# Two interleaved slabs whose last operand tile comes last in a two-block transformer kernel, and the fourth norm's squares summed two tiles later

## The chip, the cores and the metric

The program runs on one NeuronCore of a Trainium2 chip, as one launch. The metric is its device time in microseconds (us), from which a median of several executions is given. The profile is of one execution, and its span reaches from the first to the last instruction of the program. The engines are called as the profile calls them: PE is TensorE (its weight loads are PEld), DVE is VectorE, ACT is ScalarE, SP issues the DMAs of the weights.

## What is computed

Two transformer-like blocks, one after the other, on 512 tokens of width 1024, in float32. Cut to what matters here:

```python
# block 1
h = rmsnorm(x, norm_mix_pre); proj = h @ w_in
y_attn = sliding_window_attention(q, k, v, sinks, rel_bias) @ w_attn_branch
z = gelu(s5_ssm(u, ...)); z = z * sigmoid(z @ w_glu)
y_ssm = z @ w_ssm_branch
merged = sigmoid(g_attn) * y_attn + sigmoid(g_ssm) * y_ssm
x = x + rmsnorm(merged @ w_out, norm_mix_post)
h = rmsnorm(x, norm_mlp_pre)
x = x + rmsnorm(square(relu(h @ w_ff_in)) @ w_ff_out, norm_mlp_post)
# block 2
xn = rmsnorm(x, norm_mix_g_2)       # LRU branch, banded attention, gates
x = x + merged_2 @ w_out_2
xn2 = rmsnorm(x, norm_ffn_g_2)      # the fourth norm, "n4"
x = x + (silu(gate) * up) @ w_ffn_out_2
return rmsnorm(x, norm_final_g_2)
```

## The kernel before

All activations lie transposed, with channels on the 128 partitions and the 512 tokens along the free axis, in chunks of 128 channels. Every float32 product is made of three fp32r matmuls, high by high, high by low and low by high, so every operand exists as a rounded high part and a low part that holds the rest. `a_hi`/`a_lo` and `h_hi`/`h_lo` hold the activations, eight chunks each; ACT writes the high part and DVE, behind it, the low part and a count on `h_lo_ready` or `a_lo_ready`.

Weights stream in as 232 slabs of 128 by 1024 (eight 128x128 tiles). SP loads a slab into `raw`, ACT rounds it to `w_hi` (L475), DVE writes the rest to `w_lo` (L897). The pair of these is called `split`. Four slabs are in flight (`RING`), and ACT may round slab n once PE has finished slab n-4 (`half_done`).

`gemm` is PE's basic step: it waits for the slab's `w_lo`, then for the PSUM bank of its output to be free, then goes through the tiles, three matmuls of 128x512 each (L1556, L1557, L1558). With `ready` it waits ahead of each tile for that chunk of the operand. An output's bank is one of the two of `gp`, in turn. It is free when the engine that reads the output before last has counted up `out_read`; `freed_by(name, k)` is the count that has to be reached. That counter is one for the whole program and rises in program order. An operand chunk is often made from an output itself: the last chunk's low part is written at the end of a chain of PE output, DVE, ACT, DVE.

Three places matter here.

- `branch_s` (the multiplication by `w_ssm_branch`, four slabs with two outputs of four tiles each). Its operand is z times a sigmoid, from the two slabs of `glu` ahead of it. DVE makes a chunk with L1218, which also counts the bank of that `glu` output as read, and its low part with L941. Afterwards DVE and ACT work on each output in turn: L1225 (DVE, reads the bank), L1228 (DVE), L683 (ACT), L934 (DVE), and per slab one `split`. The next stage, `out`, uses the results.
- `ff`, part 0 of 4. Eight slabs (eight outputs) give the hidden chunks, each by L1293 (DVE, reads the bank, counts `out_read`), L1282 (DVE), L709 (ACT, high part), L941 (DVE, low part). The first four outputs were made together in a stage ahead (`START = 4`). Then eight slabs multiply these eight chunks, the first of them with `ready`; in part 0 their outputs are copied out by DVE at L1307.
- `n4`, the fourth norm. Squares of x are summed on ACT (L486) and DVE (L911), and PE sums them over partitions in two steps of four tiny matmuls, `first_squares` (L1579) for the first seven chunks and `last_square` (L1586) for the last. Both are done inside the first slab of `ff2`, after its tile 4. Then ACT takes the root (L494), DVE the reciprocal (L923), and PE spreads it (L1613) after tile 0 of the second slab.

DVE and ACT run in program order, so a late instruction holds up those behind it.

Of the kernel before, what the change touches and what calls it, by code (L numbers as in the profile page):

```python
# [25 lines left out]
P = 128  # L26
D = 1024
T = 512
DC = D // P
# [13 lines left out]
FF1_PART = 8  # L43
# [6 lines left out]
RING = 4  # L50
# [23 lines left out]
SLAB, _n = {}, 0  # L74
# [4 lines left out]
COUNT = dict(_counts)  # L79
# [45 lines left out]
def build(nc, slabs, params, s5p, s5bt, s5b, s5c, bias1, nd2, x_in, out):  # L125

    ctx = ExitStack()
    with ctx:
        def sb(name, shape, dt=F32):
            return ctx.enter_context(nc.sbuf_tensor(name, shape, dt))  # L130

        def sem(name):
            return ctx.enter_context(nc.semaphore(name))
# [3 lines left out]
        w_hi = sb("w_hi", [P, RING, TILES * P], F32R)  # L137
        w_lo = sb("w_lo", [P, RING, TILES * P], F32R)
# [110 lines left out]
        w_lo_ready = sem("w_lo_ready")  # L249
        half_done = sem("half_slab_done")  # L250
        out_read = sem("output_read")
# [4 lines left out]
        h_val, h_hi_ready, h_lo_ready = sem("h_value"), sem("h_hi_ready"), sem("h_lo_ready")  # L256
# [42 lines left out]
        H_AT = {"z": 0, "y1": 3, "last_z": 11, "z2": 12, "ff": 16, "xn": 48, "n4": 56}  # L299
# [45 lines left out]
        def bank(name, k):  # L345
            tensor, i = PLACE[OUT[name] + k]
            return tensor[:, i, :]

        def freed_by(name, k):

            return FREED[OUT[name] + k]
# [5 lines left out]
        class Attention:  # L357
# [3 lines left out]
            def __init__(self, first, chunk0, pairs, back, forth, q, kt, k0, v0, vt, logit, pt, sinks, name):  # L361
                self.units = [(b, pp, hp) for b in range(T // P) for pp in range(pairs) for hp in range(2)]
                self.u0, self.q, self.kt, self.k0, self.v0, self.vt = first, q, kt, k0, v0, vt
                self.logit, self.pt, self.sinks, self.name, self.pairs = logit, pt, sinks, name, pairs
                self.units_of_logit = 1.0 if name else 8.0
                self.chunks, self.done = [], []
                g = chunk0
                for b, _, _ in self.units:
                    js = [(j, b - back + j) for j in range(back + forth + 1) if 0 <= b - back + j < T // P]
                    self.chunks.append([(g + n, j, kb) for n, (j, kb) in enumerate(js)])  # L370
                    g += len(js)
                    self.done.append(g)
# [1167 lines left out]
        def _(pe):  # L1540
            def gemm(name, k, tiles, outs, x_hi, x_lo, ready=None, first=None, then={}):


                n = SLAB[name] + k
                pe.wait_ge(w_lo_ready, n + 1)
                for e in range(outs):
                    m = (outs * k if first is None else first) + e
                    dst = bank(name, m)
                    if freed_by(name, m) > 0:
                        pe.wait_ge(out_read, freed_by(name, m))  # L1550
                    for t in range(tiles):
                        if ready:
                            ready(t)
                        cols = slice((e * tiles + t) * P, (e * tiles + t + 1) * P)
                        hi, lo = w_hi[:, n % RING, cols], w_lo[:, n % RING, cols]
                        pe.matmul(dst, hi, x_hi(t), start=t == 0, stop=False)  # L1556
                        pe.matmul(dst, hi, x_lo(t), start=False, stop=False)  # L1557
                        ins = pe.matmul(dst, lo, x_hi(t), start=False, stop=t == tiles - 1)  # L1558
                        if t in then:
                            then[t]()  # L1560
                    ins.then_inc(half_done, 2 // outs)

            def a(t):
                return a_hi[:, t, :]

# [3 lines left out]
            def h(t):  # L1569
                return h_hi[:, t, :]  # L1570

            def hl(t):
                return h_lo[:, t, :]

            def first_squares(kind):

                pe.wait_ge(sq_added, ADDS * (BY_VEC[kind] + 1))
                for b in range(T // P):
                    pe.matmul(mp[:, 5, b:b + 1], ssum[:, b * P:(b + 1) * P], ones[:, 0:1], start=b == 0, stop=False,  # L1579
                              skip_group_check=True)  # L1580

            def last_square(kind):

                pe.wait_ge(sq_done, 8 * NORM[kind] - PAIRED + DC)
                for b in range(T // P):
                    ins = pe.matmul(mp[:, 5, b:b + 1], sq[(DC - 1) % 2][:, b * P:(b + 1) * P], ones[:, 0:1], start=False,  # L1586
                                    stop=True, skip_group_check=True)
                ins.then_inc(rms_sum, 1)

            def mean_square(kind):  # L1590
                first_squares(kind)
                last_square(kind)
# [16 lines left out]
            def spread(kind):  # L1609

                pe.wait_ge(rms_inverted, NORM[kind] + 1)
                for b in range(T // P):
                    ins = pe.transpose(mp[:, 5, b * P:(b + 1) * P], by_token[:, b:b + 1].to_broadcast([P, P]), ident)  # L1613
                ins.then_inc(rms_spread, 1)

            def a_stage(name, k, ready=None, then={}):
                gemm(name, k, 8, 1, a, al, ready, then=then)

            def start_stage(name, kind, count, together=DC, then={}, at_hand=()):

                order = list(at_hand)
                order += [(c, e) for c in range(len(order) // count, together) for e in range(count)]
                order += [(c, e) for e in range(count) for c in range(together, DC)]
                for c, e in order:
                    if e == 0:
                        pe.wait_ge(a_lo_ready, A_AT[kind] + c + 1)
                    if c == 0:
                        pe.wait_ge(w_lo_ready, SLAB[name] + e + 1)
                        if freed_by(name, e) > 0:
                            pe.wait_ge(out_read, freed_by(name, e))  # L1630
                    place, cols = (SLAB[name] + e) % RING, slice(c * P, (c + 1) * P)
                    hi, lo = w_hi[:, place, cols], w_lo[:, place, cols]
                    pe.matmul(bank(name, e), hi, a(c), start=c == 0, stop=False)  # L1633
                    pe.matmul(bank(name, e), hi, al(c), start=False, stop=False)  # L1634
                    ins = pe.matmul(bank(name, e), lo, a(c), start=False, stop=c == DC - 1)  # L1635
                    if c == DC - 1:
                        ins.then_inc(half_done, 2)
                        if e in then:
                            then[e]()
# [148 lines left out]
            pe.wait_ge(h_lo_ready, H_AT["last_z"] + 1)  # L1788
            for j in range(COUNT["glu"]):
                gemm("glu", j, 4, 2, lambda t: h(4 + t), lambda t: hl(4 + t))  # L1790
            for j in range(COUNT["branch_s"]):
                gemm("branch_s", j, 4, 2, h, hl,
                     (lambda t: pe.wait_ge(h_lo_ready, H_AT["z2"] + t + 1)) if j == 0 else None)
            for k in range(DC):
                a_stage("out", k, a_wait("merged") if k == 0 else None,
                        then={5: lambda: first_squares("post1")} if k == DC - 1 else {})
# [6 lines left out]
            def ff1_part(p, last=False):  # L1803

                s0, h0 = PART1 * p, H_AT["ff"] + FF1_PART * p
                for k in range(0 if p else START, FF1_PART):
                    a_stage("ff", s0 + k, then={} if p or k > START else {1: lambda: spread("n2")})
                for m in range(DC):
                    gemm("ff", s0 + FF1_PART + m, FF1_PART, 1, h, hl,
                         (lambda t: pe.wait_ge(h_lo_ready, h0 + t + 1)) if m == 0 else None,  # L1810
                         then={5: lambda: first_squares("post2")} if last and m == DC - 1 else {})

# [64 lines left out]

            def ff2_part(part, chunks, s0):
                for k in range(2 * chunks):
                    then = {0: {4: lambda: mean_square("n4")}, 1: {0: lambda: spread("n4")}}.get(s0 + k, {})  # L1880
                    gemm("ff2", s0 + k, 8, 1, h, hl,
                         (lambda t: pe.wait_ge(h_lo_ready, H_AT["n4"] + t + 1)) if s0 + k == 0 else None, then=then)
                for m in range(TAIL if part == len(FF2_CHUNKS) - 1 else DC):
                    gemm("ff2", s0 + 2 * chunks + m, chunks, 1, a, al,
                         (lambda t: pe.wait_ge(a_lo_ready, A_AT["ff2"] + 8 * part + t + 1)) if m == 0 else None)
# [195 lines left out]
```

## Time and profile before

| | |
|---|---|
| median of 3 runs | 1454.9 us (1454.07 to 1456.72) |
| the profiled execution | 1453.19 us, span 1451.4 us |
| PE busy in the span | 1412.6 us, 97% |
| DVE, ACT busy | 885.8 us, 612.7 us |
| share of the chain that ended last | PE 83%, DVE 9%, ACT 5% |
| mean granted TensorE clock | 0.997 |

A PE row of a timeline gives start, duration, engine, line, operation, output and operands. Matmuls overlap, so the distance of two starts is the rate, not the duration. The bracket is the idle time of the engine ahead of the row, and what ended it.

### The profile page before, as it was taken

Reading aid. Unit: us, or ns where it says so; the run is one execution under the profiler, and the core shown is the slowest. Engines: PE = TensorE matmul, PEld = TensorE weight load, DVE = VectorE, ACT = ScalarE, POOL = GpSimd, SP = SyncE. Lnnn points to the kernel's source line nnn. Section 1 sums busy time; section 2 is a strip of 40 time slices with the busy share of each in tenths; the row PEclk is TensorE's granted clock in tenths of the full one; section 3 lists DMA queues with packets and bytes.
Section 4 is the critical chain, followed back from the end, with each engine's and each line's share of the span. In section 5 each row is a group of like instructions: output and inputs, shape, how many; then the busy total and the mean of one; then the engine's idle time right before and its main releaser. Section 6 shows DMA issues by size and latency. Waiting matters only on the chain.

```text
span 1451.4 us, 17505 instructions
## 1 busy us (share of the span) xinstructions
PE 1412.6 (97%) x7116; PEld 1139.0 (78%) x7116; DVE 885.8 (61%) x1305; ACT 612.7 (42%) x977; POOL 1.9 (0%) x7
## 2 busy tenths in 40 slices
PE   6999999999999999999998999999999999999997
PEld 5777777787788888887786777778878888888886
DVE  6987764757635355354767888579964443453446
ACT  5453553423312222132425777788553321331232
POOL 0000000000000000000000000000000000000000
PEclk9999999999999999999999999999999999999999
DMA  4222214231323323333131121323233333333223
GB/s 166 88 83 93 59 59 145 73 108 57 116 88 101 102 88 102 90 99 108 38 116 55 48 59 58 102 73 101 88 100 91 101 102 89 100 97 106 88 87 102
DMA packets 37583, 131.60 MB, mean 91 GB/s; under 512 B 4432, under 2 KB 6608, under 8 KB 37248
## 3 DMA queue, kind: packets, MB, share of 16 engines
q1 hardware_dynamic: 37152, 127.16, 28.9%
q0 software_dynamic: 352, 3.34, 0.6%
q8 instruction: 56, 0.92, 0.3%
q14 instruction: 23, 0.19, 0.0%
HBM read 128.39 MB, written 2.10 MB: 90 GB/s over the span
## 4 chain that ended last, share of the span: by engine, by line
PE 83%; DVE 9%; ACT 5%; issue 2%; DMA 1%; SPq 0%; DVEq 0%; ACTq 0%
PE gp L1556 23%; PE gp L1557 23%; PE gp L1558 23%; PE mp L1749 2%; PE mp L1760 2%; PE mp L1730 2%; ACT w_hi L475 2%; DVE w_lo L897 2%; PE mp L1633 1%; PE mp L1635 1%; PE mp L1634 1%; PE mp L1704 1%; PE mp L1675 1%; PE mp L1710 1%; PE mp L1649 0%
## 5 line engine op out<-in xcount | busy, mean ns | idle before, releaser
L1556 PE MATMUL gp<-h_hi,w_hi 128*128 128x512 f32 x944 | 370.0, 392 | 3.7 <-DVE h_lo L941 1.9
L1558 PE MATMUL gp<-h_hi,w_lo 128*128 128x512 f32 x944 | 367.5, 389 | 0.0
L1557 PE MATMUL gp<-h_lo,w_hi 128*128 128x512 f32 x944 | 367.5, 389 | 0.0
L897 DVE TENSOR_TENSOR w_lo<-raw,w_hi 128x1024 fp32r<-128x1024 f32 x202 | 246.4, 1222 | 136.4 <-ACT w_hi L475 135.9
L1556 PE MATMUL gp<-a_hi,w_hi 128*128 128x512 f32 x692 | 271.9, 393 | 1.7 <-DVE w_lo L897 1.6
L1557 PE MATMUL gp<-a_lo,w_hi 128*128 128x512 f32 x692 | 269.4, 389 | 0.0
L1558 PE MATMUL gp<-a_hi,w_lo 128*128 128x512 f32 x692 | 269.4, 389 | 0.0
L475 ACT ACTIVATE w_hi<-raw 128x1024 fp32r<-128x1024 f32 x202 | 211.3, 1050 | 136.9 <-PE gp L1558 70.5
L1556 PEld LDWEIGHTS gp<-h_hi,w_hi 128*128 128x128 f32 x944 | 177.2, 188 | 45.1 <-issue 4.1
L1558 PEld LDWEIGHTS gp<-h_hi,w_lo 128*128 128x128 f32 x944 | 177.2, 188 | 37.3
L1557 PEld LDWEIGHTS gp<-h_lo,w_hi 128*128 128x128 f32 x944 | 177.3, 188 | 36.0
L1556 PEld LDWEIGHTS gp<-a_hi,w_hi 128*128 128x128 f32 x692 | 129.9, 188 | 32.7 <-issue 3.3
L1558 PEld LDWEIGHTS gp<-a_hi,w_lo 128*128 128x128 f32 x692 | 129.9, 188 | 27.4
L1557 PEld LDWEIGHTS gp<-a_lo,w_hi 128*128 128x128 f32 x692 | 129.9, 188 | 26.2
L709 ACT ACTIVATE h_hi<-arena 128x512 fp32r<-128x512 f32 x32 | 20.3, 633 | 134.4 <-DVE arena L1282 134.4
L1488 DVE TENSOR_TENSOR arena<-gp,R 128x512 f32<-128x512 f32 x44 | 30.4, 692 | 69.0 <-PE gp L1558 68.9
L532 ACT ACTIVATE arena<-gp 128x512 f32<-128x512 f32 x41 | 24.5, 598 | 89.1 <-PE gp L1558 88.6
L863 ACT ACTIVATE a_hi<-arena 128x512 fp32r<-128x512 f32 x22 | 13.9, 633 | 99.5 <-DVE arena L1491 99.5
L1309 DVE TENSOR_TENSOR arena<-arena,gp 128x512 f32<-128x512 f32 x24 | 16.5, 687 | 63.4 <-PE gp L1558 63.4
L897 DVE TENSOR_TENSOR w_lo<-arena,w_hi 128x1024 fp32r<-128x1024 f32 x30 | 36.7, 1223 | 29.8 <-ACT w_hi L475 29.8
L626 ACT ACTIVATE arena<-arena 128x256 f32<-128x256 f32 (+2 forms) x96 | 50.0, 526 | 0.0
L860 ACT ACTIVATE arena<-arena 128x512 f32<-128x512 f32 x22 | 13.9, 632 | 83.6 <-DVE arena L1488 83.6
(279 smaller groups left out, 1576.7 us busy)
## 6 DMA issues: line engine op xcount, KB each, us to landing
raw<-slabs SPq DMA_DIRECT2D x202, 512.0 KB, 3.6
arena<-slabs SPq DMA_DIRECT2D x30, 512.0 KB, 3.6
arena<-x_in SPq DMA_DIRECT2D x4, 512.0 KB, 6.5
arena<-x_in POOLq DMA_DIRECT2D x1, 2048.0 KB, 8.3
out_t<-arena SPq DMA_DIRECT2D x8, 256.0 KB, 2.2
arena<-bias POOLq DMA_DIRECT2D x1, 1024.0 KB, 5.2
arena<-s5b SPq DMA_DIRECT2D x1, 512.0 KB, 9.4
arena<-s5c SPq DMA_DIRECT2D x1, 512.0 KB, 10.7
```

The source lines that it names most:

```text
L475: nc.scalar.activation(w_hi[:, n % RING, :], raw(n), ACT.Copy).then_inc(w_hi_ready, 1)
L532: nc.scalar.activation(dst, bank(name, m) if src is None else src, func, scale=scale).then_inc(out_read, 1)
L626: ins = nc.scalar.activation(L, L, ACT.Exp, bias=row[:, 1, h:h + 1], scale=1.0 / A.units_of_logit, accum_out=row[:, 4, h:h + 1])
L709: nc.scalar.activation(h_hi[:, k, :], fbuf[k % 2], ACT.Copy).then_inc(h_hi_ready, 1)
L897: TT(w_lo[:, n % RING, :], raw(n), w_hi[:, n % RING, :].bitcast(F32), ALU.subtract).then_inc(w_lo_ready, 1)
L1488: TT(tmp[e], take("ff2", s0 + 2 * c + e), R[:, :], ALU.mult).then_inc(out_read, 1)
L1556: pe.matmul(dst, hi, x_hi(t), start=t == 0, stop=False)
L1557: pe.matmul(dst, hi, x_lo(t), start=False, stop=False)
L1558: ins = pe.matmul(dst, lo, x_hi(t), start=False, stop=t == tiles - 1)
L1730: pe.matmul(A.scores(i)[:, lo:hi], A.q[rows, 4 * pp + h4, b * P:(b + 1) * P], A.kt[rows, A.k0 + pp, k_lo:k_hi], start=True, stop=True).the ...
L1749: ins = pe.transpose(mp[:, 3 + g % 2, h * P:(h + 1) * P], A.logit[u % 2][:, h, j * P:(j + 1) * P], ident)
L1760: ins = pe.matmul(mp[HD * p:HD * p + HD, 5, 0:2 * P], A.vt[:, pp, kb, HD * p:HD * p + HD], A.pt[:, j, 2 * P * p:2 * P * (p + 1)], start=x ...
```

## The change

Nothing is added or removed; PE's instructions are put in another order, and waits with them. A new helper `late_tile` takes two outputs together: all tiles but the last of the first, all tiles but the last of the second, then the last tile of the first and of the second. It is used for the first slab of `branch_s` (its two outputs) and, in part 0 of `ff`, for the first two of the eight slabs of the second half. Ahead of its first matmul PE waits for both slabs' `w_lo` and for both banks. In `ff2`'s first slab the two sums of squares move from behind tile 4 to behind tile 6.

```diff
+            def late_tile(places, tiles, x_hi, x_lo, ready):
+                for some in (range(tiles - 1), (tiles - 1,)):
+                    for n, m, dst, step in places:
+                        for t in some:
+                            ready(t)
+                            cols = slice((m + t) * P, (m + t + 1) * P)
+                            hi, lo = w_hi[:, n % RING, cols], w_lo[:, n % RING, cols]
+                            pe.matmul(dst, hi, x_hi(t), start=t == 0, stop=False)
+                            pe.matmul(dst, hi, x_lo(t), start=False, stop=False)
+                            ins = pe.matmul(dst, lo, x_hi(t), start=False, stop=t == tiles - 1)
+                        if t == tiles - 1:
+                            ins.then_inc(half_done, step)
...
-            for j in range(COUNT["branch_s"]):
-                gemm("branch_s", j, 4, 2, h, hl,
-                     (lambda t: pe.wait_ge(h_lo_ready, H_AT["z2"] + t + 1)) if j == 0 else None)
+            pe.wait_ge(w_lo_ready, SLAB["branch_s"] + 1)
+            pe.wait_ge(out_read, max(freed_by("branch_s", 0), freed_by("branch_s", 1)))
+            late_tile([(SLAB["branch_s"], 4 * e, bank("branch_s", e), 1) for e in range(2)], 4, h, hl,
+                      lambda t: pe.wait_ge(h_lo_ready, H_AT["z2"] + t + 1))
+            for j in range(1, COUNT["branch_s"]):
+                gemm("branch_s", j, 4, 2, h, hl)
...
-                for m in range(DC):
-                    gemm("ff", s0 + FF1_PART + m, FF1_PART, 1, h, hl,
+                k0 = s0 + FF1_PART
+                if p == 0:
+                    pe.wait_ge(w_lo_ready, SLAB["ff"] + k0 + 2)
+                    pe.wait_ge(out_read, max(freed_by("ff", k0), freed_by("ff", k0 + 1)))
+                    late_tile([(SLAB["ff"] + k0 + m, 0, bank("ff", k0 + m), 2) for m in range(2)], FF1_PART, h, hl,
+                              lambda t: pe.wait_ge(h_lo_ready, h0 + t + 1))
+                for m in range(0 if p else 2, DC):
+                    gemm("ff", k0 + m, FF1_PART, 1, h, hl,
...
-                    then = {0: {4: lambda: mean_square("n4")}, 1: {0: lambda: spread("n4")}}.get(s0 + k, {})
+                    then = {0: {6: lambda: mean_square("n4")}, 1: {0: lambda: spread("n4")}}.get(s0 + k, {})
```

PE's queue in `branch_s`, before: the last two matmuls of the first output's last tile, and the start of the second output, whose bank is waited for there.

```order
L1557 MATMUL gp<-h_lo,w_hi 128x512
L1558 MATMUL gp<-h_hi,w_lo 128x512
L1556 MATMUL gp<-h_hi,w_hi 128x512 [waits h_lo_ready,output_read]
L1557 MATMUL gp<-h_lo,w_hi 128x512
L1558 MATMUL gp<-h_hi,w_lo 128x512
```

The same place now: the second output's first tile, which is the fourth tile of the pass, begins without a wait for a bank.

```order
L1572 MATMUL gp<-h_lo,w_hi 128x512
L1573 MATMUL gp<-h_hi,w_lo 128x512
L1571 MATMUL gp<-h_hi,w_hi 128x512 [waits h_lo_ready]
L1572 MATMUL gp<-h_lo,w_hi 128x512
L1573 MATMUL gp<-h_hi,w_lo 128x512
```

The wait for the second output's bank now stands in front of the first output's first tile, 9 or more matmuls earlier. The first output ends with its 21st matmul of the pass, where it ended with its 12th.

PE's queue in `ff`, part 0, before: the end of the last tile of slab `k0` and the start of slab `k0 + 1`.

```order
L1556 MATMUL gp<-h_hi,w_hi 128x512 [waits h_lo_ready]
L1557 MATMUL gp<-h_lo,w_hi 128x512
L1558 MATMUL gp<-h_hi,w_lo 128x512
L1556 MATMUL gp<-h_hi,w_hi 128x512 [waits output_read,w_lo_ready]
L1557 MATMUL gp<-h_lo,w_hi 128x512
L1558 MATMUL gp<-h_hi,w_lo 128x512
```

Now, the start of the pass over both slabs (behind the last product of the first half).

```order
L1557 MATMUL gp<-a_lo,w_hi 128x512
L1558 MATMUL gp<-a_hi,w_lo 128x512
L1571 MATMUL gp<-h_hi,w_hi 128x512 [waits h_lo_ready,output_read,w_lo_ready]
L1572 MATMUL gp<-h_lo,w_hi 128x512
L1573 MATMUL gp<-h_hi,w_lo 128x512
```

The wait for the second slab's bank and its `w_lo` moved ahead by 24 matmuls, in front of the first slab; slab `k0` ends with the 45th matmul of the pass, where it ended with its 24th.

PE's queue in the first slab of `ff2`, before: tile 4, the two sums of squares, tile 5.

```order
L1558 MATMUL gp<-h_hi,w_lo 128x512
L1579 MATMUL mp<-par,arena 128x1 [waits square_added]
L1579 MATMUL mp<-par,arena 128x1 x3
L1586 MATMUL mp<-par,arena 128x1 [waits square_done]
L1586 MATMUL mp<-par,arena 128x1 x3
L1556 MATMUL gp<-h_hi,w_hi 128x512 [waits h_lo_ready]
```

And now, from tile 5 on.

```order
L1556 MATMUL gp<-h_hi,w_hi 128x512 [waits h_lo_ready]
L1557 MATMUL gp<-h_lo,w_hi 128x512
L1558 MATMUL gp<-h_hi,w_lo 128x512
L1556 MATMUL gp<-h_hi,w_hi 128x512 [waits h_lo_ready]
L1557 MATMUL gp<-h_lo,w_hi 128x512
L1558 MATMUL gp<-h_hi,w_lo 128x512
L1593 MATMUL mp<-par,arena 128x1 [waits square_added]
L1593 MATMUL mp<-par,arena 128x1 x3
L1600 MATMUL mp<-par,arena 128x1 [waits square_done]
L1600 MATMUL mp<-par,arena 128x1 x3
```

Tiles 5 and 6, six matmuls, moved in front of the sums (L1593 and L1600 are the same lines of code as L1579 and L1586, 14 lines further down).

## Rows read from the trace of the kernel before

**Rows 1.** The page, section 1, PE's line: busy us, share, instructions.

```profile
PE 1412.6 (97%) x7116; PEld 1139.0 (78%) x7116; DVE 885.8 (61%) x1305; ACT 612.7 (42%) x977; POOL 1.9 (0%) x7
```

**Rows 2.** Timeline of PE, `branch_s`: start us, duration us, instruction, idle before.

```profile
257.01 0.39 PE L1556 MATMUL gp<-h_hi,w_hi 128*128 128x512 f32 x1
...
258.82 0.39 PE L1558 MATMUL gp<-h_hi,w_lo 128*128 128x512 f32 x1
260.00 0.50 PE L1556 MATMUL gp<-h_hi,w_hi 128*128 128x512 f32 x1 [0.79 <-DVE h_lo L941]
...
263.56 0.39 PE L1556 MATMUL gp<-h_hi,w_hi 128*128 128x512 f32 x1
...
275.99 0.47 PE L1556 MATMUL gp<-h_hi,w_hi 128*128 128x512 f32 x1 [1.17 <-DVE arena L1225]
...
282.86 0.47 PE L1556 MATMUL gp<-a_hi,w_hi 128*128 128x512 f32 x1 [1.12 <-DVE w_lo L897]
```

**Rows 3.** Timeline of DVE, end of `glu` and `branch_s`.

```profile
257.88 0.68 DVE L1218 TENSOR_TENSOR arena<-arena 128x512 f32<-128x512 f32 x1
...
261.35 0.68 DVE L1225 SCALAR_TENSOR_TENSOR arena<-arena,gp 128x512 f32<-128x512 f32 x1
...
282.08 0.68 DVE L1225 SCALAR_TENSOR_TENSOR arena<-arena,gp 128x512 f32<-128x512 f32 x1
```

**Rows 4.** Timeline of PE, `ff` part 0, from the first to the second half.

```profile
379.94 0.39 PE L1558 MATMUL gp<-a_hi,w_lo 128*128 128x512 f32 x1
380.97 0.47 PE L1556 MATMUL gp<-h_hi,w_hi 128*128 128x512 f32 x1 [0.65 <-issue]
...
386.45 0.50 PE L1556 MATMUL gp<-h_hi,w_hi 128*128 128x512 f32 x1 [1.13 <-DVE h_lo L941]
...
393.28 0.39 PE L1558 MATMUL gp<-h_hi,w_lo 128*128 128x512 f32 x1
393.50 0.39 PE L1556 MATMUL gp<-h_hi,w_hi 128*128 128x512 f32 x1
```

**Rows 5.** Timeline of DVE, the same place.

```profile
384.39 0.68 DVE L1293 TENSOR_TENSOR arena<-gp,R 128x512 f32<-128x512 f32 x1
...
385.71 1.47 DVE L941 TENSOR_TENSOR h_lo<-arena,h_hi 128x512 fp32r<-128x512 f32 x2
...
393.70 0.69 DVE L1307 COPY arena<-gp 128x512 f32<-128x512 f32 x1 [3.20 <-PE gp L1558]
```

**Rows 6.** Windows: us, PE, PEld, DVE, ACT, POOL busy (instructions), granted clock, DMA share, GB/s.

```profile
250.00:300.00 50.00, 46.92 (x203) 37.49 (x202) 32.51 (x43) 19.93 (x28) 0.00 (x0) 1.00 0.30 90
784.00:786.00 2.00, 0.00 (x0) 0.00 (x0) 1.83 (x8) 0.87 (x2) 0.00 (x0) 1.00 0.00 0
788.00:790.00 2.00, 2.00 (x10) 1.46 (x10) 0.45 (x2) 1.73 (x3) 0.00 (x0) 0.50 0.61 139
```

**Rows 7.** Timeline of PE, second attention: the matmuls behind the longest later wait.

```profile
786.71 1.97 PE L1749 MATMUL mp<-par,arena 128*128 128x128 f32 x8 [2.86 <-DVE arena L1164]
```

**Rows 8.** Timeline of PE, the first products of the program.

```profile
21.85 0.79 PE L1633 MATMUL gp<-a_hi,w_hi 128*128 128x512 f32 x1 [3.60 <-DVE a_lo L932]
...
25.43 0.44 PE L1635 MATMUL gp<-a_hi,w_lo 128*128 128x512 f32 x1
```

**Rows 9.** Timeline of PE, first slab of `ff2`.

```profile
1081.86 1.05 PE L1579 MATMUL mp<-par,arena 128*128 128x1 f32 x8
1083.72 1.05 PE L1586 MATMUL mp<-par,arena 128*128 128x1 f32 x8 [0.82 <-ACT arena L486]
1084.64 0.48 PE L1556 MATMUL gp<-h_hi,w_hi 128*128 128x512 f32 x1
```

**Rows 10.** Timeline of ACT, the last square of `n4`.

```profile
1083.06 0.61 ACT L486 ACTIVATE arena<-arena 128x512 f32<-128x512 f32 x1
```

**Rows 11.** Timeline of DVE, the reciprocal and the low part ahead of it.

```profile
1083.18 0.75 DVE L943 SCALAR_TENSOR_TENSOR h_lo<-arena,par,h_hi 128x512 fp32r<-128x512 f32 x1 [0.79 <-ACT h_hi L848]
...
1085.79 0.17 DVE L923 RECIPROCAL arena<-arena 128x4 f32<-128x4 f32 x1
```

## Prediction

> **What bounds the kernel now.** I read the page first, then PE's waits, then the timelines of PE, DVE and ACT at the three places that the change touches. The page shows PE busy for 97% of the span [rows 1]: this kernel ends when PE has issued its matmuls, and whatever keeps PE from issuing is added to the time. The rate is seen in a run without a wait: from 257.01 to 258.82 us lie 8 steps, 0.227 us each [rows 2]; a slab of 24 matmuls takes 5.44 us. A wait costs a little more than itself: from 260.00 to 263.56 us there are 15 steps, 3.40 us by the rate and 3.56 us in the trace, so about 0.12 to 0.16 us goes on restarting; I take 0.12 [rows 2]. From the end of a DVE instruction that frees a bank to PE's next matmul it is 0.10 us: L1225 ends at 282.08 + 0.68 = 282.76, PE goes on at 282.86 [rows 2, 3]. From the start of an output's last matmul to the DVE instruction that reads it, 0.42 us (393.28 to 393.70) [rows 4, 5].
>
> The waits that the change is about are short: 0.79 us in `branch_s` for the last chunk's low part [rows 2], 1.13 us in `ff` [rows 4], 0.82 us of idle between the two sums in `ff2` [rows 9]. So all that it can win is under 3 us. Against it stands what the front of each pass now waits for.
>
> **`branch_s`: a bank that is read late, ahead of a chain that has no slack.** PE now waits, ahead of its first matmul, for the read of `glu`'s fourth output. That is counted by L1218, which ends at 257.88 + 0.68 = 258.56 us [rows 3]. PE starts at 258.66 instead of 257.01. The wait for the last chunk is gone then (18 matmuls lie ahead of it), and all 24 matmuls end at 258.66 + 0.12 + 5.44 = 264.22, against 263.56: by PE alone a loss of 0.7 us. But the first output is complete only with the 21st matmul, which starts at 258.66 + 0.12 + 20 x 0.227 = 263.32; DVE's L1225 can read it at 263.74. Before, it ran at 261.35 [rows 3], so it is late by 2.4 us. Does that matter? L1225 of outputs 0 and 6 starts at 261.35 and 282.08, 20.73 us apart: 6.91 us for each two outputs, in which PE needs 5.44 us [rows 3]. So the chain of DVE and ACT sets the pace of this stage from its first link on, and PE waits for it: 1.17 us at 275.99 (for an L1225) and 1.12 us at 282.86, the first matmul of `out` [rows 2]. A chain at its own pace that starts 2.4 us late ends 2.4 us late; PE then starts `out` at 285.3. Term: **+2.4 us**. Its bounds are +0.7 (if the chain caught up) and +2.7 (if a new bank wait came on top).
>
> **`ff`, part 0: the wait for the second slab's bank.** Slab `k0 + 1` uses the bank of the eighth output of the first half. DVE is behind there: PE's last matmul of that output starts at 379.94, and DVE's L1293 reads it only at 384.39, to 385.07 [rows 4, 5]. Before, PE used this time: it began slab `k0` at 380.97, did six tiles, waited to 386.45, and was through both slabs at 393.50 [rows 4]. Now it stands until 385.07 + 0.10 = 385.17. Then nothing holds it up (the low parts are all there at 385.71 + 1.47 = 387.18 [rows 5], the tiles that need the last two begin later), and 48 matmuls take 10.88 us, with the restart to 396.17. Slab `k0 + 2` wants `k0`'s bank back. That slab's last matmul, the 45th, starts at 385.17 + 0.12 + 44 x 0.227 = 395.28; DVE's copy begins at 395.70, lasts 0.69 us [rows 5], and PE goes on at 396.49, with a restart of 0.12, say 396.6. Against 393.50: **+3.1 us**. Bounds: 2.6 if the second wait and the restarts cost nothing, 3.3 if the second bank's copy, behind a `split` in DVE's queue, shows too. Behind it PE runs from slab to slab with four slabs ahead, DVE and ACT have idle time (3.20 us ahead of that copy), and nothing waits to give the loss back: what PE loses here ends the program later.
>
> **The clock.** PE's standstill in `ff` is from the end of the matmul at 379.94 to 385.17, some 4.8 us. The only idle time of a warm PE that comes near it is 2.86 us at 786.71, behind which the granted clock is 0.50 (1.2 GHz) for 788 to 790, after 1.00 for 784 to 786 [rows 6, 7]. So I expect 1.2 GHz for a stretch here. What it costs: in the program's first products, at 1.2 GHz, 8 steps take 25.43 - 21.85 = 3.58 us, against 1.81 us at the fast rate, a loss of 1.8 us [rows 8]. Part of the slow stretch can fall into the idle time itself, so the cost is from 0 to 1.8 us; I take **+1.2 us**, nearer to the upper end because the standstill is longer than the one that did it.
>
> The waits in `branch_s` are shorter, and there the granted clock stays at 1.00 through 250 to 300 us in spite of two waits over 1.1 us [rows 6]. I price it at nothing there. The Trainium skill, TensorE: Matmul & The Clock Gate, "A second HAM failure mode: psum-queue depth-cycling", tells of a kernel in which frequent short idles between groups, as it cycles through banks, made the clock fall and rise again; by that rule `branch_s`, with one more such wait, would lose a slow stretch as well and the sum would be higher by up to one more of them. The row is against it here.
>
> **`ff2`: the squares.** Before, the first sum starts at 1081.86 and takes 0.92 us (as from 1083.72 to 1084.64), to 1082.78; the second waits to 1083.72 for ACT's square, which ends at 1083.06 + 0.61 = 1083.67 [rows 9, 10]. PE stands for 0.94 us. Now six matmuls, 1.36 us, come first: the first sum runs from 1083.22 to 1084.14, and the second finds the square done. Tile 7 begins at 1085.06, after its low part (1083.18 + 0.75 = 1083.93) [rows 11]. What could go wrong is the spread that follows tile 0 of the next slab, now at about 1086.5: the reciprocal is at 1085.79 to 1085.96, put there by a `split` ahead of it and not by the sum [rows 11]; the sum now ends about 0.4 us later, and the root (0.26 us on ACT) still fits ahead of 1085.79. Margin 0.5 us. Term: **-0.9 us**, bounds -1.1 and -0.4.
>
> **Sum.** 2.4 + 3.1 + 1.2 - 0.9 = +5.8 us. The profiled execution took 1453.19 us, which gives 1459.0 for its like; it is 1.7 us under the median of the three runs, 1454.9, and the same step from the median gives **1460.7 us**.
>
> **The rivals.**
> - *The clock holds.* The same, without the 1.2: 1454.9 + 4.6 = 1459.5. For it: the slow stretch may fall into the idle time. Against it: 2.86 us sufficed once.
> - *Part of the loss is given back.* If the chain in `branch_s` catches up (+0.7) and `ff` pays only 2.6, with the clock at half of its price: 0.7 + 2.6 + 0.6 - 0.9 = +3.0, 1457.9. For it speaks only that PE waits little in `out`; the even 6.9 us of the chain speak against it.
> - *Not slower: the bank in `ff` is free early.* Were L1293 to read the eighth output as soon as it is complete, at about 380.4, PE would start at 381.2, be through both slabs at 392.2 and wait for `k0`'s copy to 392.6: 0.9 us won, and no standstill for the clock. That is 2.4 - 0.9 - 0.9 = +0.6 us, 1455.5. It decides at 382.1: a read ending before that makes the pass a gain. The row has 385.07, and DVE's queue is not touched by the change, so this needs DVE to run 3 us earlier than in the trace.
> - *More than one slow stretch of the clock,* in `ff` for twice the time or in `branch_s` too: +1.8 more, 1462.5.
>
> **How the numbers follow.** Forecast as summed 0.55, clock holds 0.22, part given back 0.12, more clock 0.08, bank free early 0.03. 0.2% is 2.9 us, about what a measurement of this kernel can tell from no change: the line is at 1457.8. The first two cases and the fourth lie above it, the third lies on it and I give it half to either side; with a little for the scatter of three runs (2.65 us from end to end): slower 0.86, same 0.12, faster 0.02. The range reaches from the third case to the fourth, 1457.9 to 1462.6.
>
> **What the changed profile would show.** In `branch_s`: PE's first matmul 1.6 us behind the end of `glu`, released by L1218; L1225 of output 0 about 2.4 us later against `glu`'s end than before, then again 6.9 us for two outputs. In `ff`: an idle stretch of PE of 4.5 to 4.9 us, ended by L1293; behind it matmuls 0.43 us apart for a while; a second, short wait at `k0 + 2` on L1307. In `ff2`: no idle time between the two sums. It would be wrong if DVE's L1293 for the eighth output came earlier, if L1225's pace broke, or if the later stages held a wait for something that PE does not set off.

## The result

The change made the kernel slower: 1460.19 us in the median of 10 executions (1457.62 to 1461.92) against 1455.37 us (1453.5 to 1456.72), a ratio of 1.0033 with a 95% interval of 1.0024 to 1.0041. That is +4.8 us (+3.5 to +6.0); forecast were 1460.7 us and +5.8 us. The profiled execution of the changed kernel has a span of 1458.3 us, 6.9 us more than that of before.

Its page has the same instruction counts; PE is busy for 97% of a longer span. PE's busy time rises by 4.5 us without more work: a matmul at half the clock counts as busy for longer (0.63 us against 0.39 in `ff`'s rows below).

```profile
PE 1417.1 (97%) x7116; PEld 1142.9 (78%) x7116; DVE 886.3 (61%) x1305; ACT 612.7 (42%) x977; POOL 1.9 (0%) x7
```

**`branch_s`.** The timeline of PE (the answer to [rows 2]): the pass begins late, then every new pair of outputs waits for L1225. The trace names nothing for the first wait ("issue"), but PE goes on 0.10 us after the end of L1218 (257.13 + 0.68 = 257.81), as forecast.

```profile
256.04 0.39 PE L1558 MATMUL gp<-h_hi,w_lo 128*128 128x512 f32 x1
257.91 0.47 PE L1571 MATMUL gp<-h_hi,w_hi 128*128 128x512 f32 x1 [1.49 <-issue]
...
263.83 0.47 PE L1556 MATMUL gp<-h_hi,w_hi 128*128 128x512 f32 x1 [0.19 <-DVE arena L1225]
...
270.74 0.47 PE L1556 MATMUL gp<-h_hi,w_hi 128*128 128x512 f32 x1 [1.20 <-DVE arena L1225]
...
284.52 0.47 PE L1556 MATMUL gp<-a_hi,w_hi 128*128 128x512 f32 x1 [1.12 <-DVE w_lo L897]
```

And the timeline of DVE (the answer to [rows 3]):

```profile
257.13 0.68 DVE L1218 TENSOR_TENSOR arena<-arena 128x512 f32<-128x512 f32 x1
...
263.00 0.69 DVE L1225 SCALAR_TENSOR_TENSOR arena<-arena,gp 128x512 f32<-128x512 f32 x1 [2.31 <-PE gp L1573]
...
269.92 0.68 DVE L1225 SCALAR_TENSOR_TENSOR arena<-arena,gp 128x512 f32<-128x512 f32 x1
...
283.74 0.68 DVE L1225 SCALAR_TENSOR_TENSOR arena<-arena,gp 128x512 f32<-128x512 f32 x1
```

The two executions do not run in step (this one is 0.75 us ahead here, a gain of the first 60 us that has nothing to do with the change), so a stretch is measured from a row that both have. From L1218 to the first L1225 it was 3.47 us [rows 3] and is 5.87: 2.40 more. DVE had nothing to do for 2.31 us in between. From then on the pace is as before: 6.92 us to the next pair, 20.74 us to output 6. From L1218 to PE's first matmul of `out` it was 24.98 us and is 27.39: **+2.41 us**.

**`ff`, part 0.** PE (the answer to [rows 4]):

```profile
381.54 0.39 PE L1558 MATMUL gp<-a_hi,w_lo 128*128 128x512 f32 x1
386.77 0.76 PE L1571 MATMUL gp<-h_hi,w_hi 128*128 128x512 f32 x1 [4.84 <-DVE w_lo L897]
387.33 0.63 PE L1572 MATMUL gp<-h_lo,w_hi 128*128 128x512 f32 x1
...
391.60 0.56 PE L1573 MATMUL gp<-h_hi,w_lo 128*128 128x512 f32 x1
391.99 0.40 PE L1571 MATMUL gp<-h_hi,w_hi 128*128 128x512 f32 x1
...
400.56 0.47 PE L1556 MATMUL gp<-h_hi,w_hi 128*128 128x512 f32 x1 [0.20 <-DVE arena L1307]
```

DVE at the same place (the answer to [rows 5]):

```profile
384.84 1.23 DVE L897 TENSOR_TENSOR w_lo<-raw,w_hi 128x1024 fp32r<-128x1024 f32 x1 [1.04 <-ACT w_hi L475]
385.99 0.68 DVE L1293 TENSOR_TENSOR arena<-gp,R 128x512 f32<-128x512 f32 x1
...
399.72 0.69 DVE L1307 COPY arena<-gp 128x512 f32<-128x512 f32 x1 [9.45 <-PE gp L1573]
```

The windows (the answer to [rows 6]): the granted clock is 0.50, that is 1.2 GHz, behind the standstill.

```profile
382.00:386.00 4.00, 0.00 (x0) 0.00 (x0) 2.92 (x5) 1.58 (x2) 0.00 (x0) 0.89 0.21 83
387.00:390.00 3.00, 3.00 (x8) 2.32 (x9) 2.65 (x4) 1.81 (x3) 0.00 (x0) 0.50 0.63 175
392.00:396.00 4.00, 4.00 (x19) 3.30 (x18) 0.00 (x0) 0.00 (x0) 0.00 (x0) 1.00 0.24 95
```

PE stands for 4.84 us. The trace puts this wait down to the slab's low part (L897), but PE goes on 0.10 us after the end of L1293 (385.99 + 0.68 = 386.67), the reader of the bank, as forecast. L897 had ended at 386.07, so it alone would have held PE for all but 0.6 us of this; no run moves one of the two waits without the other. The bank had been complete since 381.96 or so (381.54 + 0.42). DVE read it 4.0 us later because the seventh output's work and a `split` (L897) stand ahead of L1293 in its queue, and that `split` waited 1.04 us for ACT's rounding. Then 10 steps from 387.33 to 391.60 take 4.27 us, 0.43 each. From L1293's start to the third slab's first matmul it was 9.11 us [rows 4, 5] and is 14.57: **+5.46 us**.

**`ff2`, the squares.** PE (the answer to [rows 9]):

```profile
1089.63 0.39 PE L1558 MATMUL gp<-h_hi,w_lo 128*128 128x512 f32 x1
...
1091.22 0.95 PE L1593 MATMUL mp<-par,arena 128*128 128x1 f32 x8
1092.03 1.03 PE L1600 MATMUL mp<-par,arena 128*128 128x1 f32 x8
1092.92 0.48 PE L1556 MATMUL gp<-h_hi,w_hi 128*128 128x512 f32 x1
...
1094.37 0.60 PE L1627 MATMUL mp<-par,arena 128*128 128x128 f32 x4
```

And before, the two rows that [rows 9] lacks, the last matmul of tile 4 and the spread:

```profile
1081.51 0.39 PE L1558 MATMUL gp<-h_hi,w_lo 128*128 128x512 f32 x1
...
1087.45 0.60 PE L1613 MATMUL mp<-par,arena 128*128 128x128 f32 x4
```

No idle time is left between the sums, nor ahead of the spread (L1627). From the last matmul of tile 4 to the spread it was 5.94 us and is 4.74 (1089.63 to 1094.37), for the same work: **-1.2 us**.

2.41 + 5.46 - 1.2 = +6.7 us for the profiled execution. The rest of its 6.9 is not the change's: -0.75 in the first 60 us, +1.1 in a stretch at 1.2 GHz around 696 us, in a stage that both kernels have and where the earlier trace had none, and small ones. The executions differ by how many such slow stretches they have: of the 10 of the changed kernel the two with a mean granted clock of 0.992 took 1461.5 and 1461.9 us, the three with 0.996 took 1457.6 to 1458.7.

### The profile page after: what moved, and what is told of

The parts are those of the page before. It is cut to its first block, busy times and chain, and to the rows that moved or that the text cites. A ratio compares the mean times of both kernels' runs of the same rounds, so it can differ in the third digit from the quotient of the medians.

```text
span 1458.3 us, 17503 instructions
## 1 busy us (share of the span) xinstructions
PE 1417.1 (97%) x7116; PEld 1142.9 (78%) x7116; DVE 886.3 (61%) x1305; ACT 612.7 (42%) x977; POOL 1.9 (0%) x7
## 4 chain that ended last, share of the span: by engine, by line
PE 87%; DVE 7%; ACT 3%; issue 1%; DMA 1%; SPq 0%; DVEq 0%; ACTq 0%
PE gp L1556 24%; PE gp L1557 23%; PE gp L1558 23%; PE mp L1763 2%; PE mp L1774 2%; PE mp L1744 2%; DVE w_lo L897 1%; ACT w_hi L475 1%; PE mp L1647 1%; PE mp L1648 1%; PE mp L1649 1%; PE mp L1718 1%; PE mp L1689 1%; PE mp L1557 1%; PE mp L1558 1%
## 5 line engine op out<-in xcount | busy, mean ns | idle before, releaser
L1556 PE MATMUL gp<-h_hi,w_hi 128*128 128x512 f32 x920 | 360.8, 392 | 2.8 <-DVE arena L1225 2.6
L1558 PE MATMUL gp<-h_hi,w_lo 128*128 128x512 f32 x920 | 358.6, 390 | 0.0
L1557 PE MATMUL gp<-h_lo,w_hi 128*128 128x512 f32 x920 | 358.6, 390 | 0.0
L897 DVE TENSOR_TENSOR w_lo<-raw,w_hi 128x1024 fp32r<-128x1024 f32 x202 | 246.5, 1222 | 136.4 <-ACT w_hi L475 136.0
L1556 PEld LDWEIGHTS gp<-h_hi,w_hi 128*128 128x128 f32 x920 | 172.9, 188 | 42.7 <-issue 3.8
L1558 PEld LDWEIGHTS gp<-h_hi,w_lo 128*128 128x128 f32 x920 | 173.0, 188 | 36.3
L1557 PEld LDWEIGHTS gp<-h_lo,w_hi 128*128 128x128 f32 x920 | 172.9, 188 | 35.1
L897 DVE TENSOR_TENSOR w_lo<-arena,w_hi 128x1024 fp32r<-128x1024 f32 x30 | 36.7, 1223 | 29.8 <-ACT w_hi L475 29.8
```

What stands on the lines that cost most here:

```text
L897: TT(w_lo[:, n % RING, :], raw(n), w_hi[:, n % RING, :].bitcast(F32), ALU.subtract).then_inc(w_lo_ready, 1)
```

## The experiments

Besides the times, each was read in its trace by the same three stretches: L1218 to `out`, L1293 to the third slab, the first slab of `ff2`.

**1. Each part alone.** `branch_alone`, `ff_alone` and `squares_alone` are the kernel before with one hunk of the change each.

> Only the branch_s part is taken over from the change; ff and the squares stay as before. Theory (a chain of DVE and ACT at its own pace starts 2.4 us late): the first output's L1225 moves back by about 2.4 us against the end of glu, again 6.9 us for each two outputs, PE begins out 2.4 us later, time +2.4 us. Rival 1 (only PE's own late start counts, the chain catches up): +0.7 us. Rival 2 (the change costs nothing here, all of its loss is in ff): 0.

> Only the ff part is taken over. Theory (standstill until DVE has read the eighth output, then matmuls at 1.2 GHz for a stretch, then a short wait for the first slab's bank): PE idle for about 4.8 us, ended by DVE, from the end of the first half to the third slab of the second +3.1 us without and +4.3 to +5.5 us with the slow stretch; time +4.3 to +5.5. Rival (the loss is the clock's alone and the standstill is made up for by the waits that go away): +1.2 to +2.4.

> Only the move of the two sums of squares behind tile 6 is taken over. Theory (PE's stall between the sums goes, the spread finds its reciprocal): -1.2 us, no idle time of PE ahead of the second sum. Rival (the wait comes back ahead of the spread, or further on): 0.

| | us, median | before | ratio, 95% | own stretch in the trace |
|---|---|---|---|---|
| branch_alone | 1457.06 | 1454.37 | 1.0014 (1.0006 to 1.0023) | +2.41 us |
| ff_alone | 1459.27 | 1454.37 | 1.0036 (1.0022 to 1.0049) | +5.48 us |
| squares_alone | 1452.29 | 1454.37 | 0.9986 (0.9978 to 0.9995) | -1.2 us |

`branch_alone`, DVE and PE: 27.39 us from L1218 to `out`, as in the whole change.

```profile
257.41 0.68 DVE L1218 TENSOR_TENSOR arena<-arena 128x512 f32<-128x512 f32 x1
```

```profile
284.80 0.47 PE L1556 MATMUL gp<-a_hi,w_hi 128*128 128x512 f32 x1 [1.15 <-DVE w_lo L897]
```

`squares_alone`, PE: no idle time between the sums, and the spread follows without a wait.

```profile
1082.65 0.95 PE L1579 MATMUL mp<-par,arena 128*128 128x1 f32 x8
1083.46 1.03 PE L1586 MATMUL mp<-par,arena 128*128 128x1 f32 x8
...
1085.80 0.60 PE L1613 MATMUL mp<-par,arena 128*128 128x128 f32 x4
```

The rivals (a chain that catches up at 0.7 us, a loss that is the clock's alone, a squares' wait that comes back) are out. The three terms add up: by their ratios +2.0, +5.2 and -2.0 us, together +5.2, against +4.8 measured for the whole. The squares' time gained more than their stretch in the trace; more of that below.

**2. The clock by itself.** The whole change, with 18 matmuls that nobody reads ahead of `ff`'s pass:

```diff
                 if p == 0:
+                    pe.wait_ge(w_lo_ready, SLAB["ff"] + k0 + 1)
+                    pe.wait_ge(h_lo_ready, h0 + 1)
+                    for _ in range(18):
+                        pe.matmul(mp[:, 4, :], w_hi[:, (SLAB["ff"] + k0) % RING, 0:P], h(0), start=True, stop=True)
                     pe.wait_ge(w_lo_ready, SLAB["ff"] + k0 + 2)
```

> The whole change, and ahead of ff's pass 18 extra matmuls of 128x512 into a bank that nobody reads (the first slab's first tile by the first chunk), about 4.1 us, which lie inside PE's standstill of 4.8 us. They compute nothing that is used. Theory (the standstill lets the clock fall to 1.2 GHz, at a cost of 2.3 us in the changed kernel's trace): the granted clock stays at 1.00 in ff, matmuls 0.23 us apart from the first on, and the time is 2 us below that of the changed kernel, +2.8 us against before. Rival (the slow stretch has nothing to do with the standstill, or the standstill is not really idle so that the filler pushes the pass back): no gain, +4.8 us or more.

Measured: 1457.73 us against 1454.37, ratio 1.0020 (1.0012 to 1.0029), +2.9 us. PE's timeline of this kernel:

```profile
381.95 4.24 PE L1830 MATMUL mp<-h_hi,w_hi 128*128 128x512 f32 x18
386.96 0.47 PE L1571 MATMUL gp<-h_hi,w_hi 128*128 128x512 f32 x1 [0.77 <-DVE w_lo L897]
...
398.29 0.47 PE L1556 MATMUL gp<-h_hi,w_hi 128*128 128x512 f32 x1 [0.20 <-DVE arena L1307]
```

The pass from its first matmul to the third slab takes 11.33 us, where it took 13.79 in the changed kernel: the slow stretch cost 2.46 us there. PE starts at the same moment with respect to DVE (L1293 at 386.18 in this trace, 0.78 us ahead of PE's start, as without the filler), so the filler displaced nothing. The granted clock is 1.00 in all windows from 380 to 400 us. The rival is out, and what is left of `ff`'s loss, 12.11 - 9.11 = 3.00 us from L1293's start to the third slab, is the standstill with the short wait for the first slab's bank.

**3. The wait and the order apart, in `branch_s`.** The change does two things there: PE waits for both banks first, and the first output is complete later.

```diff
 branch_wait:
+            pe.wait_ge(w_lo_ready, SLAB["branch_s"] + 1)
+            pe.wait_ge(out_read, max(freed_by("branch_s", 0), freed_by("branch_s", 1)))
             for j in range(COUNT["branch_s"]):
                 gemm("branch_s", j, 4, 2, h, hl,
 branch_order, in late_tile:
                         for t in some:
+                            if t == 0:
+                                pe.wait_ge(w_lo_ready, n + 1)
+                                pe.wait_ge(out_read, bank_free)
                             ready(t)
```

> The kernel before with one thing of the change: ahead of branch_s PE waits for both banks, then takes the tiles in the old order. Theory (the 2.4 us of branch_s have two causes, the early wait and the late first output, each of which alone is mostly hidden by the wait for the last chunk that was there): PE starts 1.65 us later, the first output is complete with the 12th matmul, L1225 starts 0.35 us later against glu's end, and PE begins out 0.4 us later. Rival (the early wait alone does it): 2.4 us.

> The other half: the tiles in the new order, but the second output's bank is waited for only ahead of its own first tile. Theory: PE starts at once, never waits in the pass, the first output is complete with the 21st matmul, L1225 starts 0.6 us later against glu's end than in the kernel before, PE begins out 0.6 us later. Rival (the order alone does it): 2.4 us.

There is one execution of each, so only their traces can be read, not a difference in time. `branch_wait`, DVE and PE:

```profile
256.93 0.68 DVE L1218 TENSOR_TENSOR arena<-arena 128x512 f32<-128x512 f32 x1
```

```profile
257.71 0.47 PE L1556 MATMUL gp<-h_hi,w_hi 128*128 128x512 f32 x1 [1.49 <-issue]
...
282.29 0.47 PE L1556 MATMUL gp<-a_hi,w_hi 128*128 128x512 f32 x1 [1.13 <-DVE w_lo L897]
```

`branch_order`, DVE and PE:

```profile
256.87 0.68 DVE L1218 TENSOR_TENSOR arena<-arena 128x512 f32<-128x512 f32 x1
```

```profile
261.80 0.47 PE L1556 MATMUL gp<-h_hi,w_hi 128*128 128x512 f32 x1 [0.19 <-DVE arena L1225]
...
282.49 0.47 PE L1556 MATMUL gp<-a_hi,w_hi 128*128 128x512 f32 x1 [1.12 <-DVE w_lo L897]
```

From L1218 to `out`: 25.36 us with the wait alone (+0.38), 25.62 us with the order alone (+0.64), both as worked out. Together they cost 2.41 us. They are not additive because each eats from the same slack: the 0.9 us or so that PE lost anyway ahead of the last chunk's tile, and the 0.36 us that DVE's `split` kept L1225 from starting. Either cause is hidden in large part by these, both together are not. By the terms of the prediction the early wait makes PE 1.77 us late (1.65 and a restart), the new order completes the first output 9 steps or 2.04 us later, and the slack is 0.91 + 0.12 + 0.36 = 1.39 us: 1.77 - 1.39 = 0.38, 2.04 - 1.39 = 0.65, and 1.77 + 2.04 - 1.39 = 2.42.

**4. The same in `ff`.** `ff_wait` puts the wait for the second slab's low part and bank in front and keeps the old order; `ff_order` has the new order, and waits as `branch_order` does.

> The kernel before, with the wait for the second slab's low part and bank put ahead of the first slab in ff part 0, and the tiles in the old order. Theory (the standstill and the clock are the early wait's work, the new order adds only the short wait for the first slab's bank): PE stands for 4.8 us, matmuls at 1.2 GHz behind it, third slab of the second half 2.7 us later without and 5.0 us with the slow stretch, time +4.8 us. Rival (the order does it): +1 us or less.

> The new order in ff, but the second slab's low part and bank are waited for only ahead of its own first tile. Theory: PE starts the first slab at once, waits about 1.1 us ahead of tile 6 for the seventh chunk's low part as before, no slow stretch in ff, a wait of about 0.2 us for the first slab's bank at the third slab; third slab 0.2 to 0.3 us later than before, time +0.3 us. Rival (the new order costs most of the loss): +3 us or more.

| | us, median | before | ratio, 95% | L1293 to the third slab |
|---|---|---|---|---|
| ff_wait | 1458.93 | 1455.09 | 1.0030 (1.0019 to 1.0041) | 13.11 us, +4.0 |
| ff_order | 1456.04 | 1455.09 | 1.0003 (0.9994 to 1.0013) | 9.36 us, +0.25 |

`ff_wait`, DVE and PE. Here the trace names L1293 itself as what ended the standstill.

```profile
384.09 0.68 DVE L1293 TENSOR_TENSOR arena<-gp,R 128x512 f32<-128x512 f32 x1
```

```profile
384.87 0.76 PE L1556 MATMUL gp<-h_hi,w_hi 128*128 128x512 f32 x1 [4.85 <-DVE arena L1293]
...
397.20 0.39 PE L1556 MATMUL gp<-h_hi,w_hi 128*128 128x512 f32 x1
```

`ff_order`, DVE and PE:

```profile
383.93 0.69 DVE L1293 TENSOR_TENSOR arena<-gp,R 128x512 f32<-128x512 f32 x1
```

```profile
386.00 0.50 PE L1574 MATMUL gp<-h_hi,w_hi 128*128 128x512 f32 x1 [1.14 <-DVE h_lo L941]
...
393.29 0.47 PE L1556 MATMUL gp<-h_hi,w_hi 128*128 128x512 f32 x1 [0.20 <-DVE arena L1307]
```

So in `ff` nearly all of the loss is the early wait's, with the clock that it drags along; the order costs a quarter of a microsecond. It also wins nothing: PE still waits 1.14 us ahead of tile 6. The chunk that is late is not the last but the last but one, whose low part is written just ahead of the last's ([rows 5], the row with x2), and a pass that leaves only the last tile to the end meets it in the same place. `ff_wait` was expected at 5.0 us in this stretch and had 4.0: its slow stretch was shorter than the changed kernel's. From its first matmul to the third slab it is 12.33 us, against 11.0 for 48 steps at the fast rate with a restart, so the clock cost 1.3 us here. Its time, +4.4 us by the ratio (2.8 to 6.0), is too uncertain to tell 4.0 from 5.0.

**5. A version from this.** Six tiles of each slab, then the last two of each; the second slab's waits stand ahead of its own first tile; the squares stay moved; `branch_s` is as it was. The cut shows the helper against the changed kernel's; `last` is a new argument, here 2.

```diff
-                for some in (range(tiles - 1), (tiles - 1,)):
+                for some in (range(tiles - last), range(tiles - last, tiles)):
                     for n, m, dst, step, bank_free in places:
                         for t in some:
+                            if t == 0:
+                                pe.wait_ge(w_lo_ready, n + 1)
+                                pe.wait_ge(out_read, bank_free)
...
-                              lambda t: pe.wait_ge(h_lo_ready, h0 + t + 1))
+                              lambda t: pe.wait_ge(h_lo_ready, h0 + t + 1), 2)
```

> branch_s as before the change; the squares moved as in the change; in ff part 0 the pass over two slabs leaves the last two tiles of each to the end (6 + 6 + 2 + 2), and the second slab's low part and bank are waited for only ahead of its own first tile. Theory (PE needs the second slab's bank at 385.17 us of the trace before, and six tiles of the first slab fill just that time; the low parts of chunks 7 and 8 are there before they are needed; the first slab's bank is read in time because it ends six matmuls earlier): no wait over 0.1 us in the pass but the one ahead of it, third slab 1.5 us earlier than before, with the squares' 1.2 us and fewer slow stretches there 3 us or more in all, time 1451.5 us. Rival (the wait for the seventh chunk only moves on): -2 us, the squares alone.

Measured: 1451.46 us against 1456.26, ratio 0.9970 (0.9958 to 0.9981), -4.4 us (-6.1 to -2.8). DVE and PE of this kernel:

```profile
383.95 0.69 DVE L1293 TENSOR_TENSOR arena<-gp,R 128x512 f32<-128x512 f32 x1
```

```profile
380.54 0.47 PE L1574 MATMUL gp<-h_hi,w_hi 128*128 128x512 f32 x1 [0.66 <-issue]
...
391.66 0.39 PE L1556 MATMUL gp<-h_hi,w_hi 128*128 128x512 f32 x1
```

No row between the two has idle time ahead of it. L1293 to the third slab is 7.71 us, 1.40 less than before. The second slab's first tile starts at 384.74, right behind the six tiles of the first and 0.10 us after the end of L1293: the bank comes free just when it is needed, with nothing to spare. With the squares' 1.2 us the traces show -2.6 us, a little less than the interval of the times allows. Where the rest comes from was not shown. The executions of the kernel before beside this run were slower (1456.26 us in the median) than those beside the first experiments (1454.37), so the forecast of 1451.5 us was met in part by luck.

The last one adds ten matmuls that nobody reads to the second attention, ahead of the wait that slowed the clock in the trace of before [rows 7]:

```diff
+                    if not A.name and u == 1:
+                        g = A.chunks[u][0][0]
+                        pe.wait_ge(pt_ready, g - 1)
+                        for _ in range(10):
+                            pe.matmul(mp[:, 3 + g % 2, :], h_hi[:, 1, 0:P], h_hi[:, 0, :], start=True, stop=True)
                     pe.wait_ge(probs_ready, A.u0 + u + 1)
```

> The same, and in the second attention 10 matmuls of 128x512 that nobody reads, ahead of PE's wait of 2.86 us for the second unit's probabilities, into the bank that the unit's first transposes write next. Theory (that wait lets the clock fall in nearly every execution, which costs 1.6 us): no stretch at 0.50 in the second attention, the matmuls behind the wait at the fast rate, from the first transposes of the values to the first products of the recurrence gates 160.5 us instead of 162.1, time 1.6 us under the kernel without the filler, 1450 us. Rival (DVE sets the pace there, so that the clock costs nothing): the same time as without.

Measured: 1449.19 us (1448.53 to 1449.28) against 1456.26, ratio 0.9954 (0.9941 to 0.9968), about 2.3 us under `two_last`, on the same chip. The transposes behind the wait take 1.09 us instead of 1.97 [rows 7], and from the values' transposes to the first late product of the gates it is 160.50 us, against 162.07 before and 163.19 in `two_last`, whose slow stretch there was the longer one. So the filler won 1.6 us against the one trace and 2.7 against the other; DVE does not set the pace here.

```profile
781.59 2.60 PE L1763 MATMUL mp<-h_hi 128*128 128x512 f32 x10
784.55 1.09 PE L1771 MATMUL mp<-par,arena 128*128 128x128 f32 x8 [0.35 <-DVE arena L1164]
```

This is the fastest of all these kernels.

## Why the prediction was right

- *PE bounds the kernel, and a wait on it is paid in full.* Right in the traces: the stretches, with the slow stretch around 696 us, add up to the profiled span.
- *`branch_s`, +2.4.* Right in size (+2.41 in two traces, +2.0 in the time of that part alone, 0.9 to 3.3) and in its way: first L1225 2.40 us later, then the old pace. That the two causes cost 0.4 and 0.6 when apart was worked out only for the experiments, and held.
- *`ff`, +3.1 without the clock.* Right: 3.00 us in the trace with the filler (the forecast's 396.6 counts a restart behind the matmul that is compared; its own 396.49 gives +2.99); PE restarted 0.10 us after L1293, and the short wait for L1307 was there.
- *The clock, +1.2.* The sign and the place were right, the size was too small. It cost 2.46 us in the profiled execution, more than the upper bound of 1.8, which came from the first products of the program: those had only 8 steps at 1.2 GHz, here there were 11. The length differs from trace to trace, though: `ff_alone` had the same as the changed kernel, `ff_wait` 6 steps and 1.3 us. In the times the filler brought back 1.9 of 4.8 us by the two ratios, each of which is uncertain by about 1.2 us.
- *The squares, -0.9.* Mis-sized, and just outside its bound of -1.1: it is -1.2 us in the traces. Both sums with what stands between them take 1.70 us in place of 2.78, which is 1.08 us less where the forecast counted 0.94, and the first sum starts 0.23 us behind the matmul ahead of it, not 0.35. In the times it is -2.0 (-0.7 to -3.2).
- *The sum, +5.8.* Measured +4.8, within its interval of +3.5 to +6.0. The terms by the traces would be 2.4 + 3.0 + 2.5 - 1.2 = +6.7. What lies between that and 4.8 is the choice of the execution that was profiled: that of before, at 1453.19 us, is 2.2 us under the median of the 10 executions of its kernel, that of the changed kernel (1460.12 us) is at its median. That this is the work of slow stretches at other places, in varying number, is argued and not shown; the table of clocks below fits it. So the closeness of +5.8 is in part luck: the clock was taken 1.3 us too small for this trace, the squares 0.3 us too small, and the step from a quick profiled execution was carried over to the median unchanged. (The fourth case sums to 1462.5, where the range ends at 1462.6.)
- *The rule on short idles.* The Trainium skill, TensorE: Matmul & The Clock Gate, "A second HAM failure mode: psum-queue depth-cycling", tells of short idles between groups of matmuls that made the clock of another kernel swing. Read as a rule it would have had the clock fall in `branch_s`. The trace does not bear that out here: from the start of the changed kernel's `branch_s` to that of `out` there are four idle times of 1.1 to 1.5 us, the granted clock is 1.00, and matmuls stay 0.23 us apart through all of it. Next to tiny matmuls short idles were followed by a slow stretch, see the end.

## What to carry to other kernels

When one wait is gathered for several steps and moved to the front, ask of each resource in it when it comes free on the other engine's own clock, not when PE has finished with it: here a bank was complete at 380 us and read at 385. Leaving the late operand for the end pays only if it covers all the chunks that are late (here two), if the steps put in front have their own resources by then, and if nobody lives from the output that is now complete later. Where the reader of that output sets the pace of the stage, its delay is the stage's delay.

## What the runs showed of the hardware

**Slow stretches of TensorE's clock are part of the scatter.** In the 59 executions of the kernel before that were timed beside the experiments, the mean granted clock lies between 0.993 and 0.997. At 0.997 (10 of them) the median time is 1452.6 us, at 0.996 (12) 1453.9, at 0.995 (4) 1455.3, at 0.994 (26) 1455.6 and at 0.993 (7) 1456.6. The 12 traces show where, apart from `ff` and the ends of the program: in the second attention in 10, near 690 us (a sum of squares of the norm there, with a wait of 1.31 us ahead of it) in 5, at `n4`'s squares in 2 of the 7 that have them in the old place. The wait in the second attention does not always do it: in the trace of `all_with_filler` it is 2.87 us long and has no filler, and the transposes behind it take 1.10 us at a granted clock of 1.00. `two_last_filler` had a spread of 0.75 us in 5 executions, `two_last` 1.9 in 6, the kernel before 4.4 in 10 beside them; how much of that is the filler's is open.

**The clock can fall behind a stall of 0.8 us that has tiny matmuls around it.** In the trace of `branch_wait`, whose `ff2` is as before the change, the clock fell behind the two sums of squares. The windows and PE's timeline there:

```profile
1084.00:1086.00 2.00, 1.88 (x11) 1.74 (x12) 1.29 (x2) 1.78 (x4) 0.00 (x0) 0.86 0.04 8
1086.00:1090.00 4.00, 4.00 (x15) 3.13 (x15) 0.36 (x2) 0.78 (x1) 0.00 (x0) 0.64 0.41 131
```

```profile
1084.12 1.05 PE L1586 MATMUL mp<-par,arena 128*128 128x1 f32 x8 [0.82 <-ACT arena L486]
1085.04 0.47 PE L1556 MATMUL gp<-h_hi,w_hi 128*128 128x512 f32 x1
...
1086.53 0.63 PE L1557 MATMUL gp<-h_lo,w_hi 128*128 128x512 f32 x1
```

From the first sum to the spread it took 7.21 us there (1082.25 to 1089.46), against 5.59 in the trace of before: 1.6 us. PE had issued nothing but 128x1 matmuls for 2.8 us, though the trace shows it busy for most of that. It happened so in the trace of `ff_order` too (7.21 us), and not in those of before, `branch_alone`, `ff_alone`, `ff_wait` and `branch_order` (5.6): sometimes, then. In the traces with the squares moved it did not happen. That would explain a part of why this change wins 2.0 us in the times and 1.2 in a trace: 1.6 us in 2 of 7 traces are 0.5 on average. The 11 executions of `squares_alone` lie within 1.7 us, at 0.995 and above, where the 30 of before beside them lie within 4.9 us, from 0.993 up; but those of `all_with_filler`, whose squares are moved too, spread over 4.5 us. It was not tested apart.

**The name on a wait can be the second last.** The changed kernel's 4.84 us are put down to L897, which had ended 0.6 us earlier; `ff_wait`'s same standstill is put down to L1293. The first wait of `out` is put down to L897 too (284.52), though PE goes on 0.10 us after the end of L1225 (283.74 + 0.68 = 284.42). The end of the reader plus 0.10 us tells which it was.
